# Moving the clipped decay difference of a Mamba-2 scan from ScalarE to VectorE

## The chip, the cores and the metric

The kernel runs on one core of a Trainium2 chip, as one launch. The metric is the device time in microseconds (us). A core has five engines that run side by side and wait for each other through counters (semaphores): PE (TensorE, matrix products), DVE (VectorE), ACT (ScalarE), POOL (GpSimd) and SP (SyncE, which here only starts transfers). SBUF is the working memory with 128 partitions; PSUM holds the results of PE in eight banks, which DVE and ACT can read.

## The reference

One inference step of a two-layer decoder for 256 prompt tokens and 8 decode tokens: an attention layer with a dense SwiGLU, then a Mamba-2 layer with a mixture of 8 experts. The change touches only the chunked scan of the Mamba-2 layer, for the prompt: two chunks of 128 tokens, 32 heads in 4 groups of 8.

```python
cum = jnp.cumsum(jnp.moveaxis(dtf * a_neg.reshape(g, hg), 2, -1), axis=-1)
causal = jnp.tril(jnp.ones((cl, cl), dtype=bool))
seg = jnp.exp(jnp.where(causal, cum[..., :, None] - cum[..., None, :], -jnp.inf))
xdt = xf * dtf[..., None]
cb = jnp.einsum('bclgn,bcsgn->bcgls', cf, bf)
y_diag = jnp.einsum('bcghls,bcsghp->bclghp', cb[:, :, :, None] * seg, xdt)
...
y_off = jnp.einsum('bclgn,bcghpn,bcghl->bclghp', cf, h_in, jnp.exp(cum))
```

`seg` is a 128 x 128 matrix for each head and chunk: e to the power of cum(l) - cum(s) where l is not before s, and 0 elsewhere. As the sums fall with time, the difference is never positive where it counts. So the kernel clips it at 0, takes the exponential, and leaves the masking to the product with `cb`, which is masked already.

## The kernel before, in words

All data are 32-bit floats. The Mamba-2 scan is the function `group(g_)` on DVE (line 1983), a loop over `g_` on ACT (line 1581) and one on PE (line 1108), each run four times, once for a group of 8 heads. The order on each engine is written out by hand, and each engine works strictly in that order. The loop index `n` counts 16 blocks, four in each group; a block is one chunk of one half group, so four heads, and its matrices are 128 x 512.

For a block, PE spreads the running sums of four heads over all partitions into bank 6 or bank 2 (line 1134; it counts `cum_spread`). ACT then computes max(cum(s) - cum(l), 0) with four Relu instructions of 128 x 128, one for each head, since each has its own column of `wtok` as the bias (line 1589; `seg_min`). It then takes Exp with scale -1 over the whole block (line 1594; `seg_exp`). For each odd block it also takes Exp of bank 2 (line 1598; `ecum_exp`), which PE needs before that bank can be filled again. DVE multiplies the block by the masked `cb` into `gseg` (line 2003, in `weigh(n)`), and after each odd block also forms `coff` (line 2006).

In each group DVE first scales the tokens into `xdt` (line 1992, five of them) and copies two results of PE out of bank 7 (lines 1996 and 1997). Then come the four `weigh(n)`. Between and behind them stand calls of `state_output(n)`: each is two products (line 1964) and two reductions (line 1965), of 128 x 512, for the decode tokens. There are 4, 6, 6 and 0 of these calls in groups 0 to 3. The group ends with four instructions on line 2041 and one on line 2049, which wait for the two `y_done` of PE. The first `state_output` also waits for the transfers of the rows `srow` and `feat` (`rows_spread`).

PE, in each group, turns tokens (line 1114, which waits for `y_ready` of the group before, that is for line 2041 on DVE), computes `cb` (lines 1117 and 1119), spreads the sums of two blocks (line 1134), computes one output chunk of z (line 1066, 16 products), spreads the sums of the other two blocks, forms the states (lines 1141 to 1148), computes the next z chunk, then y in two halves (lines 1161 to 1163; each half waits for its `seg_ready` and `coff_ready` from DVE, the first also for `hin` from ACT), and computes a last z chunk. ACT takes the SiLU of each z chunk (line 1559, in `z_act`). After group 3 come the output projection (line 991), the norm, the router and the experts (lines 1320 to 1374), whose weights SP brings into a ring of tiles; SP waits for PE to free a tile (line 518).

In ACT's rows a table load stands wherever the function changes between Silu and Exp. The profile names `dseg`, `eseg` and `gseg` as `segs`, `coff` and `ecum` as `convbuf`, and `hin` as `dtbuf`, as these are views of those tiles.

Of the kernel before, what the change touches and what calls it, by code (L numbers as in the profile page):

```python
# [15 lines left out]
ALU = mybir.AluOpType  # L16
ACT = mybir.ActivationFunctionType
# [3 lines left out]
P = 128  # L21
# [18 lines left out]
HG = SH // SG  # L40
# [129 lines left out]
def build(nc, a, o):  # L170
# [116 lines left out]
    wtok = sb("wtok", [P, 9, SH], c=c3)  # L287
# [1127 lines left out]
    def _(act):  # L1415
        f = act.activation
# [160 lines left out]
        f(decay, decay, ACT.Exp).then_inc(s["us_silu"], 1)  # L1577
        act.wait_ge(s["xs_turned"], 1)
        f(xtok, bank[2][:, 0:P], ACT.Copy).then_inc(s["xs_copied"], 1)
        act.wait_ge(s["out_done"], 112)  # L1580
        for g_ in range(SG):
            for n in range(4 * g_, 4 * g_ + 4):
                half, t = (n % 4) // 2, n % 2
                act.wait_ge(s["cum_spread"], n + 1)
                if n >= 2:
                    act.wait_ge(s["seg_exp"], n - 1)
                for q in range(4):
                    hh = HG * g_ + 4 * half + q
                    ins = f(dseg[:, n % 2, q, :], bank[(6, 2)[t]][:, q * P:(q + 1) * P], ACT.Relu, bias=wtok[:, 5 + t, hh:hh + 1], scale=-1.0)
                ins.then_inc(s["seg_min"], 1)  # L1590
                if n >= 2:
                    act.wait_ge(s["seg_ready"], n - 1)
                act.wait_ge(s["seg_min"], n + 1)
                f(eseg[:, n % 2], dseg[:, n % 2], ACT.Exp, scale=-1.0).then_inc(s["seg_exp"], 1)
                if n % 2:
                    if n > 1:
                        act.wait_ge(s["coff_ready"], n // 2)
                    f(ecum, bank[2][:].rearrange("p (q t) -> p q t", q=4), ACT.Exp).then_inc(s["ecum_exp"], 1)
                if n % 4 == 1:
                    z_act(*Z_AMID[g_][0])  # L1600
            act.wait_ge(s["carry_done"], 2 * g_ + 1)
            f(hin, bank[7][:], ACT.Copy).then_inc(s["hin_copied"], 1)
            act.wait_ge(s["carry_done"], 2 * g_ + 2)
            if g_:
                act.wait_ge(s["hlast_out"], 16 * g_)
            f(hout, bank[3][:].rearrange("p (q n) -> p q n", q=4), ACT.Copy).then_inc(s["hlast_copied"], 1)
            act.wait_ge(s["hlast_copied"], g_ + 1)
            act.dma_start(o[6][0, 0, HG * g_:HG * (g_ + 1)].rearrange("(q j) p n -> (j p) q n", j=2), hout).then_inc(s["hlast_out"], 16)
            z_act(*Z_AMID[g_][1])
            z_act(*Z_AMID[g_][2])  # L1610
            act.wait_ge(s["zy_ready"], g_ + 1)
            for c in range(4 * g_, 4 * g_ + 4):
                ins = f(sz[:, c, 0:TP], xcT[:, c, 0:TP], ACT.Copy, scale=vec[:, V_SNG + c:V_SNG + c + 1])
            ins.then_inc(s["gained"], 1)
# [69 lines left out]
    def _(v):  # L1684
# [298 lines left out]
        def group(g_):  # L1983
# [13 lines left out]
            v.tensor_tensor(cbT, bank[7][:, 2 * P:4 * P].rearrange("p (t n) -> p t n", t=2), mid(cst[:, C_U:C_U + P], 2), ALU.mult).then_inc(s["cb_ready"], 1)  # L1997
            v.wait_ge(s["cb_ready"], g_ + 1)

            def weigh(n):  # L2000
                half, t = (n % 4) // 2, n % 2
                v.wait_ge(s["seg_exp"], n + 1)
# [3 lines left out]
                    v.tensor_tensor(coff[:, half], ecum, mid(bcT[:, SG + g_, P:TP], 4), ALU.mult).then_inc(s["coff_ready"], 1)  # L2006

            n0 = 4 * g_
            if g_ == 0:
                weigh(n0)  # L2010
                weigh(n0 + 1)
                for n in range(3):
                    state_output(n)
                weigh(n0 + 2)
# [2 lines left out]
            elif g_ < 3:  # L2017
                state_output(6 * g_ - 2)
                weigh(n0)
                state_output(6 * g_ - 1)  # L2020
                weigh(n0 + 1)
                state_output(6 * g_)
                weigh(n0 + 2)
                weigh(n0 + 3)
# [6 lines left out]
                    v.tensor_tensor(ysp[:], ysp[:], bc(decay, [P, NB, IC]), ALU.mult).then_inc(s["ys_ready"], 1)  # L2031
            else:
                weigh(n0)
                weigh(n0 + 1)
                weigh(n0 + 2)
                weigh(n0 + 3)
            for half in range(2):
# [276 lines left out]
```

## Time and profile before

| what | value |
|---|---|
| median of 3 runs | 1746.16 us (1738.31 to 1746.92) |
| profiled execution, its own time | 1746.16 us |
| span of the profiled execution | 1744.6 us |
| PE busy | 1638.3 us (94%) |
| DVE busy | 420.6 us (24%) |
| ACT busy | 277.4 us (16%) |
| share of the last chain of work | PE 85%, DVE 7%, DMA 3%, ACT 2% |

The span is what the trace covers; 1.6 us of the execution lie around it. "Busy" is the time in which an engine worked on an instruction. The granted clock is the part of full speed that PE was given: 1.00 is 2.4 GHz and 0.50 is 1.2 GHz. The four groups of the scan lie between about 749 and 861 us of the span.

### The profile page before, as it was taken

The page shows a single profiled execution, that of the slowest core. Times are in us where ns is not written, and L with a number is a line of the kernel's source. Part 1 is how long each engine was busy: PE and PEld are TensorE (multiplying, and loading weights), DVE is VectorE, ACT ScalarE, POOL GpSimd, SP SyncE. Part 2 cuts the span into 40 slices and gives each one's busy share as a digit, 9 for nine tenths or more (in the row PEclk, how much of TensorE's full clock was granted, in tenths as well). Part 3 has the DMA queues.
Part 4 walks back from the last instruction along what each step waited for, and adds up shares of the span by engine and source line. Part 5 has one row for each costly group of instructions (what it writes and reads, how often), then busy time and mean ns, then how long its engine had stood idle before and what let it go on. Part 6 is the DMA issues. An engine that isn't in the chain of part 4 may idle for free.

```text
span 1744.6 us, 20839 instructions
## 1 busy us (share of the span) xinstructions
PE 1638.3 (94%) x8060; PEld 1042.4 (60%) x8060; DVE 420.6 (24%) x984; ACT 277.4 (16%) x615; POOL 112.8 (6%) x190
## 2 busy tenths in 40 slices
PE   7999897799999999998898999999999999999993
PEld 4555563478888878787786544554445454544452
DVE  2233432220000035679556100010001000010002
ACT  2212322210000022345413000000000000100001
POOL 0001404100000010020011000000000000010001
PEclk9999998899999999989899799999999999999996
DMA  9655974154433564545269699999999999999996
GB/s 357 259 185 195 317 246 114 34 177 144 145 115 118 173 210 124 154 126 181 77 223 361 223 335 387 386 383 388 381 393 387 379 379 394 384 380 389 392 387 232
DMA packets 255210, 462.88 MB, mean 265 GB/s; under 512 B 13423, under 2 KB 112780, under 8 KB 252005
## 3 DMA queue, kind: packets, MB, share of 16 engines
q1 hardware_dynamic: 240848, 415.02, 66.7%
q0 software_dynamic: 11760, 45.38, 8.2%
q8 instruction: 64, 1.05, 0.2%
q10 hardware_dynamic: 2512, 1.23, 0.2%
q14 instruction: 26, 0.21, 0.0%
HBM read 445.15 MB, written 16.63 MB: 265 GB/s over the span
## 4 chain that ended last, share of the span: by engine, by line
PE 85%; DVE 7%; DMA 3%; issue 2%; ACT 2%; SPq 1%; POOLq 0%; POOL 0%; DVEq 0%; ACTq 0%
PE bank L1320 18%; PE bank L991 10%; PE bank L1362 9%; PE bank L1018 9%; PE bank L1335 9%; PE bank L1374 5%; PE bank L1032 5%; PE bank L731 2%; PE bank L821 1%; PE bank L768 1%; PE bank L739 1%; DVE ysp L1965 1%; DVE prod L1964 1%; PE bank L1066 1%; PE bank L826 1%
## 5 line engine op out<-in xcount | busy, mean ns | idle before, releaser
L1320 PE MATMUL bank<-ring,hg 128*128 128x512 f32 (+1 forms) x624 | 254.7, 566 | 0.7 <-ACT hg L1645 0.7
L1320 PEld LDWEIGHTS bank<-ring,hg 128*128 128x128 f32 x624 | 119.1, 192 | 132.0 <-issue 129.6
L1018 PE MATMUL bank<-hT,ring 128*128 128x264 f32 x704 | 156.9, 386 | 1.3 <-ACT hT L1431 1.3
L1018 PEld LDWEIGHTS bank<-hT,ring 128*128 128x128 f32 x704 | 133.7, 190 | 24.9 <-issue 2.1
L2228 DVE TENSOR_TENSOR actH<-sgH,bank 128x512 f32<-128x512 f32 (+1 forms) x24 | 15.4, 643 | 465.7 <-PE bank L1320 465.7
L1362 PE MATMUL bank<-ring,turnH 128*128 128x512 f32 x256 | 115.8, 605 | 3.3 <-ACT turnH L1670 3.3
L991 PE MATMUL bank<-hT,ring 128*128 128x264 f32 x512 | 117.4, 390 | 1.6 <-ACT hT L1431 1.3
L991 PEld LDWEIGHTS bank<-hT,ring 128*128 128x128 f32 x512 | 98.2, 192 | 19.6 <-issue 2.1
L1335 PE MATMUL bank<-ringx,hg 128*64 128x256 f32 x832 | 93.0, 381 | 0.0
L1362 PEld LDWEIGHTS bank<-ring,turnH 128*128 128x128 f32 x256 | 47.9, 192 | 68.7 <-issue 67.8
L1032 PE MATMUL bank<-actT,ring 128*128 128x264 f32 x352 | 79.1, 386 | 0.6 <-DVE actT L1868 0.6
L1335 PEld LDWEIGHTS bank<-ringx,hg 128*64 128x64 f32 x832 | 58.5, 137 | 32.2 <-issue 4.1
L1032 PEld LDWEIGHTS bank<-actT,ring 128*128 128x128 f32 x352 | 66.8, 190 | 12.4 <-DVE actT L1868 1.0
L1658 ACT ACTIVATE sgH<-bank 128x512 f32<-128x512 f32 (+1 forms) x24 | 13.5, 562 | 374.9 <-PE bank L1320 374.9
L1374 PE MATMUL bank<-ring,turnL 128*64 128x512 f32 x288 | 67.7, 612 | 0.8 <-DVE turnL L2244 0.8
L1335 PE MATMUL bank<-ring,hg 128*64 128x256 f32 (+1 forms) x704 | 65.0, 342 | 0.0
L1066 PE MATMUL bank<-hT,ring 128*128 128x264 f32 x256 | 64.9, 412 | 0.0
L991 PE MATMUL bank<-sz,ring 128*128 128x264 f32 x256 | 60.0, 394 | 3.6 <-DVE sz L2060 3.6
L1066 PEld LDWEIGHTS bank<-hT,ring 128*128 128x128 f32 x256 | 51.1, 204 | 10.6 <-issue 1.4
L991 PEld LDWEIGHTS bank<-sz,ring 128*128 128x128 f32 x256 | 49.7, 194 | 12.8 <-DVE sz L2060 4.0
L1320 PE MATMUL bank<-ringx,hg 128*128 128x512 f32 (+1 forms) x144 | 56.4, 545 | 0.0
L1665 ACT ACTIVATE sgL<-bank 128x256 f32<-128x256 f32 (+1 forms) x24 | 8.8, 366 | 298.1 <-PE bank L1335 298.1
(509 smaller groups left out, 1846.5 us busy)
## 6 DMA issues: line engine op xcount, KB each, us to landing
ring<-in_moe_w_down SPq DMA_DIRECT2D x70, 1024.0 KB, 12.7
ring<-in_moe_w_up SPq DMA_DIRECT2D x59, 1024.0 KB, 11.4
ring<-in_moe_w_gate SPq DMA_DIRECT2D x55, 1024.0 KB, 11.5
ring<-in_w_ada SPq DMA_DIRECT2D x48, 1024.0 KB, 8.9
ringx<-in_moe_w_gate SPq DMA_DIRECT2D x37, 1024.0 KB, 11.0
ringx<-in_moe_w_up SPq DMA_DIRECT2D x33, 1024.0 KB, 12.0
ring<-in_ssm_w_in SPq DMA_DIRECT2D x20, 1024.0 KB, 5.3
ringx<-in_moe_w_down SPq DMA_DIRECT2D x20, 1024.0 KB, 12.3
```

What stands on the lines that cost most here:

```text
L731: m = mm(b_[rows, :], scT[:, 4 * u + k, :], slot4(n + u)[:, k, :], start=u == 0, stop=u == 1, skip_group_check=True)
L739: m = mm(out[q], adaS[:, u, q * P:(q + 1) * P], cst[:, C_SEL:C_SEL + 9], start=True, stop=True)
L768: m = mm(out, slot8(n)[:, k, (m_ % 2) * P:(m_ % 2) * P + width], hT[:, k, :], start=k == 0, stop=k == DC - 1)
L821: m = mm(bank[h % 2][0:QK, 0:T], wqb[:, k, h * QK:(h + 1) * QK], projT[:, k, :], start=k == 0, stop=k == QC - 1)
L991: m = mm(bank[n % 4][:, 0:T], w[:, k, (n % per_tile) * P:(n % per_tile + 1) * P], rhs[:, k, :], start=k == 0, stop=k == kc - 1)
L1018: m = mm(bank[2 * w + q][:, 0:T], slot8(tl)[:, k, q * P:(q + 1) * P], hT[:, k, :], start=k == 0, stop=k == DC - 1)
L1032: m = mm(bank[2 * (j % 2) + q][:, 0:T], slot8(tl)[:, kk, q * P:(q + 1) * P], actT[:, k0 + kk, :], start=k == 0 and kk == 0, stop=k == 3 an ...
L1066: m = mm(bank[n % 2][:, 0:T], slot8(tl)[:, k, (n % 2) * P:(n % 2 + 1) * P], hT[:, k, :], start=k == 0, stop=k == DC - 1)
L1320: m = mm(bank[b_][:, 0:width], hg[:, k, 0:CAPH], w[:, kk, :], start=k == 0, stop=k == DC - 1)
L1335: m = mm(bank[2][64 * v_:64 * v_ + 64, 256 * b_:256 * b_ + width // 2], hg[:, k, CAPH:CAPS], w[:, kk, v_], start=k == 0, stop=k == DC - 1, ...
L1362: m = mm(bank[4 + half][:, :], turnH[:, 2 * i + q, :], w[:, q, 512 * half:512 * (half + 1)], start=g == 0 and i == 0 and q == 0, stop=g == ...
L1374: m = mm(bank[6][64 * v_:64 * v_ + 64, :], turnL[:, i, 64 * q:64 * q + 64], w[:, q, 512 * v_:512 * (v_ + 1)], start=g == 0 and i == 0 and ...
```

## The change

The clipped difference goes from ACT to DVE. ACT loses its 64 Relu instructions and waits for `seg_min` from DVE; its Exp no longer has the scale -1, as DVE writes min(cum(l) - cum(s), 0). ACT's one wait for `out_done` goes too; DVE has the same wait ahead of its first group. DVE gains a function `seg(n)` with four TENSOR_SCALAR instructions of 128 x 128 from PSUM (subtract a column of `wtok`, then min with 0), and each group calls it four times: for the first two blocks behind line 1997, for the third behind the first `weigh`, for the fourth behind the second `weigh`. The waits on `cum_spread` and on `seg_exp` (of two blocks before) go with it to DVE.

```diff
@@ ACT
-        act.wait_ge(s["out_done"], 112)
         for g_ in range(SG):
             for n in range(4 * g_, 4 * g_ + 4):
-                half, t = (n % 4) // 2, n % 2
-                act.wait_ge(s["cum_spread"], n + 1)
-                if n >= 2:
-                    act.wait_ge(s["seg_exp"], n - 1)
-                for q in range(4):
-                    hh = HG * g_ + 4 * half + q
-                    ins = f(dseg[:, n % 2, q, :], bank[(6, 2)[t]][:, q * P:(q + 1) * P], ACT.Relu, bias=wtok[:, 5 + t, hh:hh + 1], scale=-1.0)
-                ins.then_inc(s["seg_min"], 1)
+                act.wait_ge(s["seg_min"], n + 1)
                 if n >= 2:
                     act.wait_ge(s["seg_ready"], n - 1)
-                act.wait_ge(s["seg_min"], n + 1)
-                f(eseg[:, n % 2], dseg[:, n % 2], ACT.Exp, scale=-1.0).then_inc(s["seg_exp"], 1)
+                f(eseg[:, n % 2], dseg[:, n % 2], ACT.Exp).then_inc(s["seg_exp"], 1)
@@ DVE
+            def seg(n):
+                half, t = (n % 4) // 2, n % 2
+                v.wait_ge(s["cum_spread"], n + 1)
+                if n >= 2:
+                    v.wait_ge(s["seg_exp"], n - 1)
+                for q in range(4):
+                    hh = HG * g_ + 4 * half + q
+                    ins = v.tensor_scalar(dseg[:, n % 2, q, :], bank[(6, 2)[t]][:, q * P:(q + 1) * P], wtok[:, 5 + t, hh:hh + 1], 0.0,
+                                          ALU.subtract, ALU.min)
+                ins.then_inc(s["seg_min"], 1)
...
             n0 = 4 * g_
+            seg(n0)
+            seg(n0 + 1)
             if g_ == 0:
                 weigh(n0)
+                seg(n0 + 2)
                 weigh(n0 + 1)
+                seg(n0 + 3)
                 for n in range(3):
                     state_output(n)
                 weigh(n0 + 2)
...
             elif g_ < 3:
                 state_output(6 * g_ - 2)
                 weigh(n0)
+                seg(n0 + 2)
                 state_output(6 * g_ - 1)
                 weigh(n0 + 1)
+                seg(n0 + 3)
                 state_output(6 * g_)
...
             else:
                 weigh(n0)
+                seg(n0 + 2)
                 weigh(n0 + 1)
+                seg(n0 + 3)
                 weigh(n0 + 2)
                 weigh(n0 + 3)
```

PE's order is the same in both. On DVE in group 0, from the last copy out of bank 7 to the first `state_output` (lines 1964 and 1965), stands before:

```order
L1997 TENSOR_TENSOR usbuf<-bank,cst 128x256
L2003 TENSOR_TENSOR segs<-segs,usbuf 128x512 [waits seg_exp,cb_ready]
L2003 TENSOR_TENSOR segs<-segs,usbuf 128x512 [waits seg_exp]
L2006 TENSOR_TENSOR convbuf<-convbuf,bcT 128x512 [waits ecum_exp]
L1964 TENSOR_TENSOR prod<-st,srow 128x512 [waits st_loaded0,rows_spread]
L1965 TENSOR_REDUCE ysp<-prod 128x4 [waits dve_step]
```

In the changed kernel (where line 1998 is `seg`, 2005 and 2008 are `weigh`, 1955 and 1956 are `state_output`) the same place reads:

```order
L1988 TENSOR_TENSOR usbuf<-bank,cst 128x256
L1998 TENSOR_SCALAR segs<-bank,wtok 128x128 [waits cum_spread,cb_ready]
L1998 TENSOR_SCALAR segs<-bank,wtok 128x128 x3
L1998 TENSOR_SCALAR segs<-bank,wtok 128x128 [waits cum_spread]
L1998 TENSOR_SCALAR segs<-bank,wtok 128x128 x3
L2005 TENSOR_TENSOR segs<-segs,usbuf 128x512 [waits seg_exp]
L1998 TENSOR_SCALAR segs<-bank,wtok 128x128 [waits seg_exp,cum_spread]
L1998 TENSOR_SCALAR segs<-bank,wtok 128x128 x3
L2005 TENSOR_TENSOR segs<-segs,usbuf 128x512 [waits seg_exp]
L2008 TENSOR_TENSOR convbuf<-convbuf,bcT 128x512 [waits ecum_exp]
L1998 TENSOR_SCALAR segs<-bank,wtok 128x128 [waits seg_exp,cum_spread]
L1998 TENSOR_SCALAR segs<-bank,wtok 128x128 x3
```

All four `seg` now stand ahead of the first `state_output`, and the last two wait for the third and fourth `cum_spread` of PE.

On ACT in group 0, from the SiLU of a z chunk on, stands before:

```order
L1559 ACT_TABLE_LOAD
L1559 ACTIVATE sz<-bank 128x264 [waits units]
L1589 ACTIVATE segs<-bank,wtok 128x128 [waits seg_exp,cum_spread]
L1589 ACTIVATE segs<-bank,wtok 128x128 x3
L1594 ACT_TABLE_LOAD [waits seg_min]
L1594 ACTIVATE segs<-segs 128x512 [waits seg_ready]
L1589 ACTIVATE segs<-bank,wtok 128x128 [waits seg_exp,cum_spread]
L1589 ACTIVATE segs<-bank,wtok 128x128 x3
L1594 ACTIVATE segs<-segs 128x512 [waits seg_min,seg_ready]
```

and in the changed kernel (line 1585 is the Exp):

```order
L1559 ACT_TABLE_LOAD
L1559 ACTIVATE sz<-bank 128x264 [waits units]
L1585 ACT_TABLE_LOAD [waits seg_ready]
L1585 ACTIVATE segs<-segs 128x512 [waits seg_min]
L1585 ACTIVATE segs<-segs 128x512 [waits seg_ready,seg_min]
```

The number of table loads is the same; the load for Exp no longer waits for `seg_min`.

## Rows read from the trace of the kernel before

**Rows 1.** Stretches of the four groups: busy time (instructions) by engine, PE clock, DMA

```profile
749.00:777.00 28.00, 27.57 (x161) 23.33 (x160) 21.44 (x34) 13.70 (x30) 6.57 (x11) 0.82 0.55 143
777.00:805.00 28.00, 23.50 (x164) 20.02 (x162) 26.84 (x43) 16.77 (x37) 1.59 (x3) 0.97 0.60 190
805.00:833.00 28.00, 24.10 (x162) 20.52 (x161) 26.96 (x43) 16.63 (x35) 1.44 (x2) 0.93 0.36 117
833.00:861.00 28.00, 27.54 (x157) 23.00 (x155) 9.47 (x18) 16.81 (x35) 0.55 (x1) 0.80 0.18 50
```

**Rows 2.** Timeline of DVE, group 2: start, us, operation, [idle before]

```profile
811.59 0.69 DVE L2003 TENSOR_TENSOR segs<-segs,usbuf 128x512 f32<-128x512 f32 x1
812.20 0.68 DVE L1964 TENSOR_TENSOR prod<-st,srow 128x512 f32<-128x512 f32 x1
```

**Rows 3.** Waits from 745 to 875 us: what for, us in total, times, longest

```profile
DVE segs L2003 <- ACT segs L1594: 15.1, 6, 6.3
```

**Rows 4.** Timeline of DVE, groups 0 and 3

```profile
757.25 0.68 DVE L2006 TENSOR_TENSOR convbuf<-convbuf,bcT 128x512 f32<-128x512 f32 x1
760.44 0.69 DVE L1964 TENSOR_TENSOR prod<-st,srow 128x512 f32<-128x512 f32 x1 [2.51 <-DMA feat<-xsd]
...
777.24 3.08 DVE L1992 TENSOR_TENSOR xdt<-bank,wtok 128x512 f32<-128x512 f32 x5 [0.50 <-PE bank L1114]
...
851.95 0.68 DVE L2006 TENSOR_TENSOR convbuf<-convbuf,bcT 128x512 f32<-128x512 f32 x1
```

**Rows 5.** Timeline of PE, groups 0 to 3

```profile
760.55 2.05 PE L1134 MATMUL bank<-feat,cst 32*128 32x128 f32 x16
...
770.35 0.38 PE L1163 MATMUL bank<-convbuf,dtbuf 128*64 128x128 f32 x2
771.16 0.40 PE L1161 MATMUL bank<-segs,xdt 128*64 128x128 f32 x2 [0.43 <-DVE convbuf L2006]
...
772.87 3.83 PE L1066 MATMUL bank<-hT,ring 128*128 128x264 f32 x16
...
803.69 1.97 PE L1114 MATMUL bank<-cst,xcT 128*128 128x128 f32 x8 [4.50 <-DVE xcT L2041]
...
831.81 1.97 PE L1114 MATMUL bank<-cst,xcT 128*128 128x128 f32 x8 [3.90 <-DVE xcT L2041]
...
838.69 6.61 PE L1066 MATMUL bank<-hT,ring 128*128 128x264 f32 x16
845.23 2.04 PE L1134 MATMUL bank<-feat,cst 32*128 32x128 f32 x16
849.95 3.73 PE L1066 MATMUL bank<-hT,ring 128*128 128x264 f32 x16
```

**Rows 6.** Timeline of ACT, groups 0 and 2

```profile
761.74 1.14 ACT L1589 ACTIVATE segs<-bank,wtok 128x128 f32<-128x128 f32 x4 [0.69 <-PE bank L1134]
...
816.25 1.28 ACT L1594 ACT_TABLE_LOAD   x1
```

**Rows 7.** Groups of DVE instructions by shape: busy us, mean ns, idle before

```profile
L1896 DVE TENSOR_SCALAR dtbuf<-bank,hp_ 32x264 f32<-32x264 f32 x1 | 0.5, 480 | 1.1 <-PE bank L1051 1.1
```

**Rows 8.** Timeline of DVE: rows that give a step from start to start

```profile
830.10 1.65 DVE L2041 SCALAR_TENSOR_TENSOR xcT<-xcT,expd,bank 128x256 f32<-128x256 f32 x4
...
991.38 0.28 DVE L2159 TENSOR_SCALAR pick<-cst,slots 128x128 f32<-128x128 f32 x1
991.58 0.28 DVE L2160 TENSOR_SCALAR pick<-twice,slots 128x128 f32<-128x128 f32 x1
```

**Rows 9.** PE in three stretches: length, busy (instructions), granted clock, DMA

```profile
800.00:812.00 12.00, 8.31 (x44) 0.86 0.62 203
828.00:848.00 20.00, 16.19 (x64) 0.66 0.11 26
862.00:872.00 10.00, 7.87 (x28) 0.83 0.56 176
```

**Rows 10.** Waits of SP's queue from 700 us: us in total, times, longest

```profile
SPq L518 <- PE bank L1320: 248.3, 86, 15.6
```

## The prediction

> **What bounds the kernel now.** I first read the busy times by stretch. The page of the profile calls PE 94% busy and DVE 24%, but that is a mean over stages. In the stretches of groups 1 and 2 of the scan, DVE works 26.84 and 26.96 of 28 us while PE works 23.50 and 24.10, and ACT 16.77 and 16.63 [rows 1]. So there DVE sets the pace. In group 3, where no decode work stands on DVE, it is PE: 27.54 of 28 us, with DVE at 9.47.
>
> Next I read DVE's timeline, to see whether "busy" hides waits. In group 2 the first weigh starts at 811.59 and the next instruction at 812.20, 0.61 us on and with no idle time before it [rows 2]. The waits confirm it: over all four groups DVE stood before line 2003 only six times, 15.1 us in all [rows 3]. On the timeline two of them lie in group 0 and four in group 3, none in groups 1 and 2. Group 0 is different: DVE finishes its first coff at 757.93, then waits 2.51 us for a transfer, and starts the first state_output at 760.44 [rows 4].
>
> Then PE's timeline. In group 0 it waits for DVE's second coff and starts the second half of y at 771.16. In groups 2 and 3 it opens only after 4.50 and 3.90 us of waiting for DVE's line 2041 [rows 5]. Behind the scan, SP waits for PE to free ring tiles, 86 times for line 1320 alone, 248.3 us in total [rows 10]. The experts are thus not fed too slowly: they start late if PE comes late, and nothing behind makes it up. A delay of the scan should reach the end one for one.
>
> **The change, part by part.** ACT loses 64 Relu of 128 x 128; four of them take 1.14 us [rows 6], so about 18 us of busy time. I count that as no gain: ACT has 11 us of slack in each group [rows 1], and neither PE nor DVE waits for it in groups 1 and 2. ACT's dropped wait for the output transfers costs or gains nothing, since its first Relu waited for PE beyond it and DVE holds the same wait already. The table loads stay in number; they now precede the wait for DVE and so lie beside its work.
>
> DVE gains 64 TENSOR_SCALAR of 128 x 128 from PSUM with a scalar column. The trace has no such shape; I need the step from one start to the next. Above: 256 columns from PSUM with a scalar column take 1.65 us for four, 0.41 a step [rows 8]. The column price is (690 - 280)/384 = 1.07 ns, from 512 columns at 0.69 us [rows 2] and 128 at 0.28 us [rows 8]. So 128 columns fewer make 0.41 - 0.137 = 0.27. Second way: the same operation from PSUM, 264 columns, lasts 480 ns [rows 7]; less 136 columns that is 0.335. The 128-column row shows steps of 0.20 at a duration of 0.28 [rows 8], so a step is 0.08 below the duration: 0.255. Below lies the SBUF step itself, 0.20. I take 0.26, from the same operation, so 1.04 us for one seg (0.80 to 1.34 with the full duration as the step).
>
> On that last bound the Trainium skill bears ("VectorE: DVE Perf Modes", section "The DRAIN you can't avoid"): the next operation does not start until the pipe is empty. By that a seg would cost four durations, 1.34 us. The trace of before speaks against it for unchained operations, with 0.20 from start to start at a duration of 0.28 [rows 8].
>
> Group 0. seg of blocks 0 and 1 fits into DVE's old wait for ACT. The third seg needs PE's third spread: ACT's Relu on it started at 761.74, having waited for PE [rows 6], and PE's sixteen products there run from 760.55 to 762.60 [rows 5]. PE gets there no sooner. On DVE's queue this wait now holds up the weigh and coff of block 1, the fourth seg, and all state_outputs. So: seg at 761.74, to 762.78; weigh and coff at 0.61 each, to 764.00; fourth seg to 765.04. The first state_output starts there and not at 760.44: +4.60 us. The transfer it waited for [rows 4] has landed by then. Everything DVE does in the group follows, then PE's second half of y, then PE's transposes. DVE waited 0.50 us for these before 777.24 [rows 4], so PE is last there and the delay passes on whole.
>
> Groups 1 and 2. Each has four seg on a DVE without idle time: 4 x 1.04 = 4.16 us each, +8.32. No wait comes with them: PE is ahead of DVE there, as its 4 us of slack show [rows 1], and ACT finishes each Exp behind a 2.9 us state_output.
>
> Group 3. Four more seg, 4.16 us, but hidden. PE ends its middle z chunk at 849.95 + 3.73 = 853.68 [rows 5], DVE its last coff before at 852.63 [rows 4]. With the change: third spread done at about 846.25 [rows 5], seg 847.3, weigh and coff 848.5, fourth seg 849.6, Exp 850.3, then weigh and coff to 851.6. That is 2 us before PE needs it; if the cover went it would cost up to 4.2.
>
> PE's clock. PE's wait before the second half of y in group 0 grows from 0.43 us to 775.76 - 770.73 = 5.0 us [rows 5]. Around the waits of 4.50 and 3.90 us, and one after 860 us, the mean granted clock was 0.86 over 12 us, 0.66 over 20 and 0.83 over 10 [rows 9]. As only 0.50 and 1.00 occur, that is 3.4, 13.6 and 3.4 us at 1.2 GHz. So I expect a slow stretch behind the new wait. A short one takes at most 3.4/2 = 1.7 us from the work that follows, part of it falling into the wait; I take 1.1, and it is exposed, since PE is last there. Group 3 I leave as it was.
>
> This is also what the Trainium skill says ("TensorE: Matmul & The Clock Gate", "Part 1: The HAM clock gate"): throttled is the default, and activity releases it. The trace agrees in all three places above.
>
> Sum: 4.60 + 8.32 + 1.1 = 14.0 us. The profiled execution took 1746.16 us, 1.6 over its span of 1744.6, and is the median of the three runs itself. So 1760 us, +0.8%. The third run, at 1738.31, shows that one execution can come out 8 us shorter.
>
> **The rivals.**
> A, a long slow clock behind the new wait: 13.6 us as in group 3 instead of 3.4. PE's work from 771.16 to 776.7 (half of y, a z chunk) then takes twice as long, +5.4 in place of 1.1, giving 12.9 + 5.4 = 18.3 us, 1764 us. For it: 16 products of line 1066 took 6.61 us in group 3 and 3.73 at full clock [rows 5]. Against: two of three stretches were short.
>
> B, the clock goes the other way: group 3 opens with a short slow stretch where before it had the long one. PE sets the pace there, so (13.6 - 3.4)/2 = 5.1 us come back; with seg at 0.80 the DVE terms are 4.12 + 6.40. Then 10.5 + 1.1 - 5.1 = 6.5 us, 1753 us. For it: when the clock falls and returns differs from gap to gap. Against: it takes both.
>
> C, the delay is taken up later: prefetch stands full anyway, or a later wait for a transfer shrinks by as much. That would be 1747 to 1750 us. Against: SP's waits for PE [rows 10].
>
> D, ACT paces the groups and DVE's state_outputs only fill: then each of groups 0 to 2 loses two Relu blocks (2 x 1.14 us) and one exposed table load (1.28) [rows 6], 3.56 us each, 10.7 together: 1735.5 us, faster. It decides if DVE waits for Exp inside groups 1 and 2. Against: all its waits there are in groups 0 and 3 [rows 3], and the starts stand back to back [rows 2].
>
> E, the pipe empties between the seg instructions: 1.34 us a seg. Group 0 costs 2.52 + 2.68 = 5.2, groups 1 and 2 10.7, with the clock 17.0 us, 1763 us. The skill's page on draining would have it so.
>
> **How the numbers follow.** Forecast 0.55 (its own range 1756 to 1763), A 0.13, B 0.12, C 0.07, D 0.05, E 0.08. Half a per cent is 8.7 us, about what a measurement of this kernel can tell from no change; so slower means above 1754.9. Slower: 0.55 + 0.13 + 0.08 and a third of B, 0.80. Same: the rest of B and C, 0.15. Faster: D, 0.05. The range, 1751 to 1767 us, runs from just below B to above A and E, and leaves out C and D, and the case that A and E come together with more waits.
>
> **What would show it.** DVE's line 1998: 64 instructions, 0.33 to 0.35 us each, four in about 1.1. The first state_output near 765.0. PE's second half of y in group 0 near 775.8, with about 5 us of idle time before it. Groups 1 and 2 together longer by 8.3 us, and DVE without idle time in both. Group 3 no longer than before but for its clock. The forecast is wrong if DVE shows idle time inside groups 1 and 2, if a step is under 0.20, if PE arrives in group 0 earlier than at 760.55, or if the experts begin less late than the scan ends late.

## The result, and the profile after

The changed kernel took 1754.56 us in the median of its 17 runs (1748.22 to 1759.22), against 1745.25 us for 17 runs of the kernel before on the same chip, one of which came out at 1963.56 us and is left out of the comparison. The ratio is 1.0059, with a 95% interval of [1.0045, 1.0075]: the change makes the kernel slower, by 0.59% or 10.3 us (0.0059 x 1745; the medians as they stand are 9.3 apart). In a later series the same pair gave 1756.94 us (4 runs) and 1743.94 us (23 runs), a ratio of 1.0081 [1.005, 1.0112]. The prediction was 1760 us, in a range from 1751 to 1767.

The profiled execution has a span of 1755.5 us, against 1744.6 before. Its busy times and its instructions, from the page:

```profile
PE 1636.9 (93%) x8060; PEld 1042.4 (59%) x8060; DVE 437.4 (25%) x1048; ACT 260.7 (15%) x551; POOL 112.9 (6%) x190
```

DVE gained 64 instructions and 16.8 us, ACT lost 64 and 16.7 us. That says nothing of the path. The next view is the busy times of the four groups, each from DVE's first `xdt` to that of the next group (columns: stretch, length, then PE, PEld, DVE, ACT, POOL with their instructions, granted clock, DMA share, GB/s):

```profile
748.40:782.80 34.40, 29.40 (x163) 24.88 (x162) 25.56 (x50) 9.58 (x15) 6.59 (x11) 0.80 0.46 134
782.80:814.60 31.80, 23.65 (x162) 19.88 (x161) 30.87 (x58) 12.28 (x19) 1.59 (x3) 0.98 0.49 147
814.60:846.70 32.10, 24.70 (x162) 20.86 (x161) 31.11 (x60) 12.47 (x19) 1.44 (x2) 0.93 0.34 103
846.70:874.50 27.80, 27.23 (x157) 22.76 (x155) 13.63 (x34) 12.48 (x19) 0.55 (x1) 0.81 0.18 50
```

In groups 1 and 2, DVE is busy for 30.87 of 31.80 and 31.11 of 32.10 us, so it still sets the pace and every added us lengthens them. In group 3, PE is busy for 27.23 of 27.80, as before [rows 1]. Group by group, between the same landmarks on DVE's timeline (from the first `xdt` to that of the next group; group 3 ends where DVE's last product over 1024 columns of `xcT` and `sz` starts, at 861.07 us before and 874.46 after):

| us | group 0 | group 1 | group 2 | group 3 | sum |
|---|---|---|---|---|---|
| before | 28.21 | 27.68 | 28.11 | 28.04 | 112.04 |
| after | 34.40 | 31.81 | 32.06 | 27.76 | 126.03 |
| difference | +6.19 | +4.13 | +3.95 | -0.28 | +13.99 |

DVE's timeline, groups 0 and 1 (start, us, operation, idle time before it in brackets), shows how these come about:

```profile
761.14 1.13 DVE L1998 TENSOR_SCALAR segs<-bank,wtok 128x128 f32<-128x128 f32 x4 [5.30 <-PE bank L1134]
762.18 0.68 DVE L2005 TENSOR_TENSOR segs<-segs,usbuf 128x512 f32<-128x512 f32 x1
762.78 0.69 DVE L2008 TENSOR_TENSOR convbuf<-convbuf,bcT 128x512 f32<-128x512 f32 x1
763.38 1.12 DVE L1998 TENSOR_SCALAR segs<-bank,wtok 128x128 f32<-128x128 f32 x4
764.42 0.68 DVE L1955 TENSOR_TENSOR prod<-st,srow 128x512 f32<-128x512 f32 x1
...
782.83 3.08 DVE L1983 TENSOR_TENSOR xdt<-bank,wtok 128x512 f32<-128x512 f32 x5 [2.13 <-PE bank L1114]
...
786.60 2.16 DVE L1998 TENSOR_SCALAR segs<-bank,wtok 128x128 f32<-128x128 f32 x8
788.68 0.68 DVE L1955 TENSOR_TENSOR prod<-st,srow 128x512 f32<-128x512 f32 x1
```

The first `state_output` starts at 764.42, where before it stood at 760.44 [rows 4]. PE's third spread came 0.60 us sooner in this execution (759.95 against 760.55 [rows 5]), so against PE the delay is 3.98 + 0.60 = 4.6 us. Eight clip instructions in a row take 788.68 - 786.60 = 2.08 us from start to start, which is 0.26 us each, or 1.04 a `seg`. At the end of group 0, DVE waits 2.13 us for PE's transposes where it had waited 0.50 [rows 4]. PE's timeline of that place says why:

```profile
759.95 2.04 PE L1134 MATMUL bank<-feat,cst 32*128 32x128 f32 x16
...
775.13 0.40 PE L1161 MATMUL bank<-segs,xdt 128*64 128x128 f32 x2 [5.00 <-DVE convbuf L2008]
...
778.01 4.27 PE L1066 MATMUL bank<-hT,ring 128*128 128x264 f32 x16
782.12 1.04 PE L1114 MATMUL bank<-cst,xcT 128*128 128x128 f32 x8
```

PE waited 5.00 us instead of 0.43 and then worked at a lower clock for a while: the z chunk behind it took 4.27 us and not 3.83 [rows 5], and the half of y before it from 775.13 to 778.01, 2.88 us, against 772.87 - 771.16 = 1.71 before. The granted clock of two stretches there, and of one in group 3:

```profile
772.00:776.00 4.00, 0.87 (x10) 0.90 (x12) 3.90 (x7) 0.00 (x0) 0.00 (x0) 0.94 1.04 362
776.00:780.00 4.00, 4.00 (x25) 3.38 (x22) 3.86 (x8) 0.00 (x0) 0.55 (x1) 0.63 0.21 33
848.00:852.00 4.00, 4.00 (x19) 3.78 (x19) 3.57 (x9) 1.72 (x4) 0.55 (x1) 0.50 0.05 16
```

With 0.50 and 1.00 as the only levels, the first two hold (0.06 + 0.37) x 8 = 3.4 us at 1.2 GHz. That stretch costs 1.6 us (2.13 - 0.50, and 1.17 + 0.44 on PE). It began only when PE was at work again: from 775.0 to 775.5 us the granted clock was still 1.00, from 775.6 to 778.9 it was 0.50. The waits from 745 to 875 us (us in total, times, longest) have the new ones:

```profile
ACT segs L1585 <- DVE segs L1998: 27.5, 14, 5.6
...
DVE segs L1998 <- PE bank L1134: 12.3, 5, 5.6
...
PE bank L1161 <- DVE convbuf L2008: 7.7, 3, 5.0
...
PE bank L1161 <- ACT dtbuf L1593: 3.3, 2, 2.2
```

The last two rows also hold waits of PE inside groups 1 and 2 which the kernel before did not have: 2.17 and 1.16 us for ACT's `hin`, and 1.35 us in each for DVE's `coff`. They cost nothing, since DVE is last in these groups.

In group 3 the clip waits for PE's third spread too, as ACT's did before, but nothing is late behind it. DVE and then PE at that place:

```profile
859.81 1.13 DVE L1998 TENSOR_SCALAR segs<-bank,wtok 128x128 f32<-128x128 f32 x4 [5.61 <-PE bank L1134]
...
864.48 0.68 DVE L2008 TENSOR_TENSOR convbuf<-convbuf,bcT 128x512 f32<-128x512 f32 x1
```

```profile
845.48 1.97 PE L1114 MATMUL bank<-cst,xcT 128*128 128x128 f32 x8 [4.88 <-DVE xcT L2051]
...
863.34 3.73 PE L1066 MATMUL bank<-hT,ring 128*128 128x264 f32 x16
```

DVE ends its last `coff` at 865.16, PE its middle z chunk at 867.07: 1.9 us of slack. The kernel before had 1.05 there (852.63 against 853.68): with the clip on DVE, the last `coff` is done 18.5 us after the group's start and not 19.6.

Behind the scan the two executions differ once more. The span grew by 10.9 us and not by 14. The scan started 0.6 us sooner, and what lies behind it took 2.5 us less. The kernel before had two stretches of 3.4 us at 1.2 GHz in its experts and the changed one had none; at half their length they make up 3.4 us, so 0.9 us went the other way and were not traced. The 16 products of line 1362 hold the first of these stretches; PE in the kernel before, and after:

```profile
991.46 8.63 PE L1362 MATMUL bank<-ring,turnH 128*128 128x512 f32 x16 [0.88 <-ACT turnH L1670]
```

```profile
1004.83 7.11 PE L1362 MATMUL bank<-ring,turnH 128*128 128x512 f32 x16 [0.88 <-ACT turnH L1661]
```

These products start 1004.83 - 991.46 = 13.37 us later, and the scan ended 874.46 - 861.07 = 13.39 us later: up to there nothing made the delay up.

### The profile page after: what moved, and what is told of

It reads as the page before. It is cut to its first block, busy times and chain, and to the rows that moved or that the text cites. A ratio compares the mean times of both kernels' runs of the same rounds, so it can differ in the third digit from the quotient of the medians.

```text
span 1755.5 us, 20835 instructions
## 1 busy us (share of the span) xinstructions
PE 1636.9 (93%) x8060; PEld 1042.4 (59%) x8060; DVE 437.4 (25%) x1048; ACT 260.7 (15%) x551; POOL 112.9 (6%) x190
## 3 DMA queue, kind: packets, MB, share of 16 engines
q8 instruction: 64, 1.05, 0.3%
## 4 chain that ended last, share of the span: by engine, by line
PE 86%; DVE 8%; DMA 2%; issue 2%; ACT 1%; SPq 1%; POOLq 0%; POOL 0%; DVEq 0%; ACTq 0%
PE bank L1320 17%; PE bank L991 10%; PE bank L1018 9%; PE bank L1362 9%; PE bank L1335 9%; PE bank L1374 5%; PE bank L1032 4%; PE bank L731 2%; PE bank L821 1%; PE bank L768 1%; PE bank L1066 1%; DVE ysp L1956 1%; DVE prod L1955 1%; PE bank L739 1%; PE bank L826 1%
## 5 line engine op out<-in xcount | busy, mean ns | idle before, releaser
L2238 DVE TENSOR_TENSOR actH<-sgH,bank 128x512 f32<-128x512 f32 (+1 forms) x24 | 15.4, 644 | 463.7 <-PE bank L1320 463.7
L991 PEld LDWEIGHTS bank<-hT,ring 128*128 128x128 f32 x512 | 98.2, 192 | 19.6 <-issue 2.1
L1335 PEld LDWEIGHTS bank<-ring,hg 128*64 128x64 f32 x704 | 45.5, 137 | 17.6 <-issue 2.3
## 6 DMA issues: line engine op xcount, KB each, us to landing
ringx<-in_moe_w_up SPq DMA_DIRECT2D x33, 1024.0 KB, 13.6
ringx<-in_moe_w_down SPq DMA_DIRECT2D x20, 1024.0 KB, 13.7
```

What stands on the lines that cost most here:

```text
L991: m = mm(bank[n % 4][:, 0:T], w[:, k, (n % per_tile) * P:(n % per_tile + 1) * P], rhs[:, k, :], start=k == 0, stop=k == kc - 1)
L1335: m = mm(bank[2][64 * v_:64 * v_ + 64, 256 * b_:256 * b_ + width // 2], hg[:, k, CAPH:CAPS], w[:, kk, v_], start=k == 0, stop=k == DC - 1, ...
```

## The experiments

The kernels marked with "before" start from the kernel before, the others from the changed one. Ratios are taken against the kernel before in the same batch, on the same chip (1744.82 us for x1, x2, x3 and y1, 1743.19 for x6, b2, x9 and y4, 1743.94 for w1 and y5), so kernels of different batches are better compared by their ratios. The lengths of the groups, from the profile of each, in the same way as above:

| kernel | group 0 | group 1 | group 2 | group 3 | sum | median us | ratio |
|---|---|---|---|---|---|---|---|
| x1_order | 30.20 | 31.73 | 32.06 | 28.08 | 122.07 | 1751.5 | 1.0041 [1.0024, 1.0057] |
| x2_act12 | 34.38 | 27.59 | 28.09 | 23.48 | 113.54 | 1742.54 | 0.9987 [0.9962, 1.0012] |
| x3_keep | 33.55 | 31.71 | 31.96 | 22.14 | 119.36 | 1749.53 | 1.0027 [1.0013, 1.0041] |
| y1_shift (before) | 29.69 | 24.70 | 24.69 | 22.66 | 101.74 | 1729.45 | 0.9911 [0.9882, 0.9939] |
| x6_g3 | 29.67 | 27.62 | 28.07 | 23.39 | 108.75 | 1743.1 | 1.0003 [0.9981, 1.0025] |
| b2_keep (before) | 28.39 | 27.60 | 27.85 | 22.20 | 106.04 | 1733.38 | 0.9935 [0.9912, 0.9958] |
| x9_double | 34.30 | 35.96 | 38.15 | 27.69 | 136.10 | 1765.01 | 1.0124 [1.009, 1.0158] |
| y4_keep (before) | 31.37 | 24.70 | 24.69 | 22.51 | 103.27 | 1729.89 | 0.9919 [0.9892, 0.9947] |
| w1_both | 31.36 | 28.81 | 28.80 | 28.18 | 117.15 | 1742.56 | 0.9992 [0.997, 1.0014] |
| y5_out (before) | 29.82 | 24.68 | 24.68 | 22.54 | 101.72 | 1732.76 | 0.9925 [0.9899, 0.995] |

### Group 0: the wait alone (x1_order)

The same work, with the third and fourth `seg` later on DVE's queue:

```diff
                 weigh(n0)
-                seg(n0 + 2)
                 weigh(n0 + 1)
+                state_output(0)
+                seg(n0 + 2)
+                state_output(1)
                 seg(n0 + 3)
-                for n in range(3):
-                    state_output(n)
+                state_output(2)
```

> Changed kernel with another order on DVE in group 0 alone: both weigh first, then state_output(0), the third seg, state_output(1), the fourth seg, state_output(2). If the 4.6 us of group 0 are a wait for PE's third spread (2.5 us) plus two seg (2.08 us), only the two seg remain: the first state_output starts when its transfer has landed, 4.0 us earlier than in the changed kernel, DVE has no 5.3 us of idle time before a seg there, group 1 starts 2.5 us earlier, and the time is about 1752 us. If group 0 costs by DVE's load alone, the order changes nothing and the time stays at 1754.5.

Group 0 fell from 34.40 to 30.20 us, by 4.2. DVE and PE at the same places:

```profile
757.05 0.69 DVE L1955 TENSOR_TENSOR prod<-st,srow 128x512 f32<-128x512 f32 x1 [2.49 <-DMA feat<-xsd]
...
759.95 1.13 DVE L1998 TENSOR_SCALAR segs<-bank,wtok 128x128 f32<-128x128 f32 x4
...
775.91 3.08 DVE L1983 TENSOR_TENSOR xdt<-bank,wtok 128x512 f32<-128x512 f32 x5 [0.50 <-PE bank L1114]
```

```profile
769.84 0.40 PE L1161 MATMUL bank<-segs,xdt 128*64 128x128 f32 x2 [1.36 <-DVE convbuf L2008]
...
771.54 3.83 PE L1066 MATMUL bank<-hT,ring 128*128 128x264 f32 x16
```

`seg` no longer waits, DVE is back at the old 2.49 us of waiting for the transfer, PE waits 1.36 us in place of 5.00, and its z chunk takes 3.83 us. So 2.5 us of group 0's 6.2 were the wait, 1.6 the clock behind PE's wait, and the 2.0 that stay (30.20 - 28.21) are the two `seg` that no cover hides.

### Groups 1 and 2: the work alone (x2_act12, x9_double)

x2_act12 gives the clip of groups 1 and 2 back to ACT, with the wait on `cum_spread` and the four Relu as they were before:

```diff
             for n in range(4 * g_, 4 * g_ + 4):
+                on_act = g_ in (1, 2)
+                if on_act:
...
             def seg(n):
+                if g_ in (1, 2):
+                    return
```

> Changed kernel with the clip of groups 1 and 2 back on ACT as Relu; groups 0 and 3 stay on DVE. If the 32 seg instructions of groups 1 and 2 lie on the path at 0.26 us each, 8.3 us go: about 1746 us, and each of the two groups takes 4.16 us less. If DVE's load there is hidden and the loss comes from group 0 or from PE's clock, the time stays at 1751 us or above.

Both groups returned to their old lengths, by 4.22 and 3.97 us. The row of group 1 is that of before again, with DVE at 26.68 of 27.60 us and ACT at 16.48:

```profile
782.90:810.50 27.60, 23.04 (x163) 19.56 (x161) 26.68 (x42) 16.48 (x35) 1.59 (x3) 0.99 0.55 169
...
838.60:862.10 23.50, 22.95 (x157) 19.41 (x155) 13.51 (x34) 12.47 (x19) 0.55 (x1) 0.96 0.20 59
```

Group 3 was 4.3 us shorter than after, with a granted clock of 0.96 in place of 0.81: the slow stretch at its opening was a short one here. That is rival B's event, and it was not asked for. The median fell by 12 us where 8.3 were expected, and the profile shows where the rest can come from: 4.3 us in group 3, and 4.4 us behind the scan, where a slow stretch of 17.1 us at the router, which both kernels of the pair had, was missing. So the lengths of groups 1 and 2 are the evidence here, and not the median.

x9_double has DVE do each clip of groups 1 and 2 a second time, into `gseg`, which is overwritten later:

```diff
                                           ALU.subtract, ALU.min)
+                if g_ in (1, 2):
+                    for q in range(4):
+                        hh = HG * g_ + 4 * half + q
+                        ins = v.tensor_scalar(gseg[:, half, t, q, :], bank[(6, 2)[t]][:, q * P:(q + 1) * P], wtok[:, 5 + t, hh:hh + 1], 0.0,
+                                              ALU.subtract, ALU.min)
```

> Changed kernel with each clip instruction of groups 1 and 2 issued twice on DVE, the second time into a buffer that is written again before it is read. If these instructions lie on the path at 0.26 us each, both groups get another 4.16 us longer: 1754.5 + 8.3 = 1763 us. If the loss came from waits and order and not from load, the time stays near 1755.

Group 1 grew by 4.15 us, as much as the first clip had cost. Group 2 grew by 6.09. The windows of its opening and rest:

```profile
812.00:828.00 16.00, 13.19 (x46) 11.27 (x46) 15.24 (x35) 6.01 (x9) 0.53 (x1) 0.57 0.41 133
828.00:854.00 26.00, 17.00 (x121) 14.10 (x120) 23.84 (x47) 6.46 (x10) 1.44 (x2) 0.95 0.31 92
```

A slow stretch of 13.7 us now stood at the opening of group 2 as well, where the changed kernel had one of 3.4; group 3 kept its own (27.69 us, granted clock 0.81). PE had four us of slack in group 2 and used them up; DVE then waited 1.50 us for PE's spread, which with the 4.16 of work makes 5.66 of the 6.09 us:

```profile
829.37 1.13 DVE L1998 TENSOR_SCALAR segs<-bank,wtok 128x128 f32<-128x128 f32 x4 [1.50 <-PE bank L1134]
```

### Group 3 and the clock (x6_g3, x3_keep, b2_keep, y4_keep)

x6_g3 has the clip on DVE in group 3 alone, and on ACT in groups 0 to 2 (and keeps ACT's wait for `out_done`).

```diff
+                on_act = g_ < 3
+                if on_act:
...
+            def seg(n):
+                if g_ < 3:
+                    return
```

> Kernel before with the clip on DVE in group 3 alone (16 of the 64 instructions), groups 0 to 2 as before. If group 3 hides them behind PE, groups 0 to 2 last as before, group 3 lasts 28.0 us at the long slow clock or some 23 us at a short one, and the time is that of the kernel before, about 1745 us. If they lie on the path, group 3 gets up to 4.2 us longer: 1749 us.

The median did not change (1.0003). Group 3 took 23.39 us, again with a short slow stretch, so its length can't be set beside 28.04. The next two can: in both, PE does unused products of 128 x 512 (line 705) while it would wait. x3_keep, on the changed kernel:

```diff
                 if t == 0 and g_ > 0:
+                    pe.wait_ge(s["seg_min"], 4 * g_)
+                    keep_clock(bank[6], 5)
                     pe.wait_ge(s["y_ready"], 2 * g_)
...
             for half in range(2):
+                if g_ == 0 and half:
+                    pe.wait_ge(s["seg_min"], 4)
+                    keep_clock(bank[6], 5)
                 pe.wait_ge(s["seg_ready"], 4 * g_ + 2 * half + 2)
```

> Changed kernel in which PE runs five unused 128 x 512 products (about 4.6 us) before it waits for DVE: in group 0 ahead of the second half of y, and at the start of groups 1 to 3. They write a free bank and are read by nobody. If the clock terms are as worked out, the granted clock stays at 1.00 through the scan, the first xdt scaling of group 1 comes 1.6 us earlier, and group 3, which PE paces, gets 5 to 6 us shorter: about 1747 us in all. If the clock costs nothing there, since DVE is last anyway, the time stays at 1754.5; if the extra products come in the way of the real ones, it rises by 1 to 3 us.

b2_keep, on the kernel before, has four of them at the opening of groups 2 and 3 only:

```diff
+                if t == 0 and g_ > 1:
+                    pe.wait_ge(s["seg_min"], 4 * g_)
+                    keep_clock(bank[6], 4)
                 if t == 0 and g_ > 0:
```

> Kernel before in which PE runs four unused 128 x 512 products (about 3.6 us) before it waits for DVE at the start of groups 2 and 3, into a free bank. If the slow clock at the start of group 3 costs 5 us of a stretch that PE paces, group 3 gets 5 us shorter and the time is about 1740 us; groups 0 to 2 stay as they are, since DVE paces them. If the clock is not on the path, the time stays at 1745 us.

Group 3, first in x3_keep, then in b2_keep:

```profile
840.50:862.60 22.10, 21.62 (x153) 18.13 (x151) 13.49 (x34) 12.47 (x19) 0.55 (x1) 1.00 0.23 64
```

```profile
827.90:850.10 22.20, 21.66 (x153) 18.18 (x151) 9.46 (x19) 16.65 (x35) 0.55 (x1) 1.00 0.24 64
```

At full clock throughout, group 3 lasts 22.14 us with the clip on DVE and 22.20 with it on ACT. So the clip of group 3 costs nothing, which is shown here with PE at its fastest. The slow stretch of group 3 cost 28.04 - 22.20 = 5.8 us in the kernel before and 27.76 - 22.14 = 5.6 in the changed one, nearly as much as the change cost in group 0.

In group 0, x3_keep gained only 0.85 us, where its expectation had more. The products at the opening of group 1 stood in the way:

```profile
771.84 4.45 PE L705 MATMUL bank<-cst 128*128 128x512 f32 x10
776.13 1.04 PE L1116 MATMUL bank<-cst,xcT 128*128 128x128 f32 x8
```

There PE is last, and the transposes (line 1116 here) started 4.3 us later than they could. Two gains stand against this loss. The clock behind the second half of y gave its 1.6 us. And PE's third spread started 8.00 us after the first `xdt` and not 11.52, because in this execution the slow stretch at the start of the scan, which the edit doesn't touch, was 3.4 us long and not 10.2; that took 3.5 us off. The edit was misplaced by me; it tells nothing against the clock. y4_keep repeats the error in small. It adds to y1_shift (below) four unused products before the second half of y in group 0 and three before the output projection:

```diff
+                if g_ == 0 and half:
+                    pe.wait_ge(s["seg_min"], 4)
+                    keep_clock(bank[6], 4)
...
+        keep_clock(bank[6], 3)
         pe.wait_ge(s["gated_vector"], 1)
```

> The kernel with 4, 5, 5 and 2 calls of state_output, and unused products on PE where it still waits: four ahead of the second half of y in group 0, three ahead of the output projection. In the run without them one slow stretch of 3.4 us stood behind each of these two waits. If both cost half their length, 3.4 us go: about 1726 us. If one of them was hidden, half of that; if neither costs, 1729.5.

It stayed level with y1_shift (1729.89 and 1729.45 us). PE's products ran from 770.76 to 774.46, while DVE's `coff` was ready at 771.14 already:

```profile
770.76 3.70 PE L705 MATMUL bank<-cst 128*128 128x512 f32 x8
774.39 0.43 PE L1164 MATMUL bank<-segs,xdt 128*64 128x128 f32 x2
```

```profile
770.45 0.69 DVE L2010 TENSOR_TENSOR convbuf<-convbuf,bcT 128x512 f32<-128x512 f32 x1
```

Group 0 took 31.37 us, against 29.69 in y1_shift. But y4_keep had the 10.2 us stretch at the start of the scan and y1_shift one of 3.4; with the long one, group 0 took 28.1 to 28.4 us in the kernels before without the insertion (profiles of before, r_before and b2_keep), so the insertion cost about 3. The equal medians hide more than this: behind the scan the profiled execution of y4_keep was 7.5 us shorter (its slow stretch at the router was 3.4 us long and not 17.1), and 4.2 us of its time lay outside the span, where y1_shift had 1.6. So this run says nothing of the second insertion. y5_out drops the first of the two insertions and keeps `keep_clock(bank[6], 3)` before the projection.

> The kernel with 4, 5, 5 and 2 calls of state_output and three unused products on PE ahead of its wait before the output projection, where nothing real is held up. The first two columns of the projection took 9.06 us behind a slow clock and 7.1 at full clock: about 2 us less than without them, 1727.5 us, if the clock stays up; 1729.5 if not. Groups 0 to 3 as in the kernel without them, 101.7 us.

The products fit into PE's wait, and the projection's first 32 products took 7.38 us, against 9.07 in y1_shift. PE in y5_out, then in y1_shift:

```profile
850.40 2.74 PE L705 MATMUL bank<-cst 128*128 128x512 f32 x6
854.16 7.38 PE L991 MATMUL bank<-sz,ring 128*128 128x264 f32 x32 [1.02 <-DVE sz L2062]
```

```profile
848.87 9.07 PE L991 MATMUL bank<-sz,ring 128*128 128x264 f32 x32 [3.59 <-DVE sz L2061]
```

No gain is left in the time: 1732.76 us where 1727.5 were expected, with a ratio whose interval overlaps that of y1_shift. In this profile the slow stretch at the router was 20.5 us long instead of 17.1, which by half of 3.4 would take the 1.7 us back; whether the one brought the other wasn't tried.

### The better versions (y1_shift, w1_both)

If DVE paces groups 1 and 2 and PE group 3, decode work should move from the former to the latter. y1_shift is the kernel before with 4, 5, 5 and 2 `state_output` in the groups, in place of 4, 6, 6 and 0; the scaling of `ysp` goes from the end of group 2 to behind the last of them:

```diff
             elif g_ < 3:
-                state_output(6 * g_ - 2)
+                first = 5 * g_ - 1
+                state_output(first)
...
-                state_output(6 * g_ + 3)
             else:
+                state_output(14)
                 weigh(n0)
                 weigh(n0 + 1)
+                state_output(15)
+                v.wait_ge(s["ys_ready"], NB)
...
```

> Kernel before with 4, 5, 5 and 2 calls of state_output in groups 0 to 3 in place of 4, 6, 6 and 0. If DVE's load sets the length of groups 1 and 2, each gets 2.9 us shorter and the two calls in group 3 are hidden beside PE: 5.8 us less, about 1739.5 us, and up to 5 more where PE's wait gets too short to drop the clock for group 3. If ACT or PE paces the groups, the time stays at 1745.

Groups 1 and 2 fell by 2.98 and 3.42 us, one `state_output` each (2.9 us; group 2 also lost the scaling of `ysp`), and group 3 by 5.4: PE's waits before groups 2 and 3 shrank to 1.61 and 1.74 us, and no slow stretch followed them.

```profile
797.34 1.09 PE L1114 MATMUL bank<-cst,xcT 128*128 128x128 f32 x8 [1.61 <-DVE xcT L2042]
...
822.03 1.09 PE L1114 MATMUL bank<-cst,xcT 128*128 128x128 f32 x8 [1.74 <-DVE xcT L2042]
```

This is the fastest kernel of the study, 0.9911 [0.9882, 0.9939] of the kernel before. w1_both puts the clip on DVE in it, with group 0 in the order of x1_order.

> The kernel with 4, 5, 5 and 2 calls of state_output and with the clip on DVE (in group 0 in the better order). If the clip costs wherever DVE paces, groups 1 and 2 last 24.7 + 4.2 = 28.9 us each and group 0 gains 2.1; in group 3, where DVE now has two state_outputs as well, up to 4 us are no longer hidden: 10 to 14 us over the 1729.5 of the kernel without the clip on DVE, so 1740 to 1744 us. If relief of ACT is worth something once DVE has less to do, it stays under 1737.

Its median is 13 us above that of y1_shift (14 by the ratios), and its scan is 15.4 us longer: 1.7, 4.1, 4.1 and 5.5 in the four groups. Group 3 is no longer free, because the clip now delays the last decode results on DVE, and PE waits for their transfer, 2.52 us where y1_shift waits 0.4, with a slow stretch behind it (5.42 us for 16 products, 3.73 in y1_shift):

```profile
854.78 0.33 PE L1167 MATMUL bank<-cst,usbuf 128*128 128x128 f32 x1 [2.52 <-DMA usbuf<-ysd]
854.95 5.42 PE L1066 MATMUL bank<-hT,ring 128*128 128x264 f32 x16
```

### The pair once more (r_after, r_before)

Both kernels unchanged, in a series of their own.

> The changed kernel once more, for a second profile. Its four groups lasted 126.0 us in the first, 14.0 more than before, but the time rose by only 10.3. If the scan differs from execution to execution by the length of PE's slow stretches, the sum of groups 0 to 2 stays within 2 us of 98.3, as DVE paces them, and group 3 is either near 28 or near 23 us. If the 14 us were a chance of one profile, the groups 1 and 2 move too.

> The kernel before once more, for a second profile. Groups 1 and 2 stay at 27.7 and 28.1 us, group 0 at 28 to 30, group 3 near 28 or near 23 us by the length of the slow stretch at its start.

The scan took 125.89 and 112.05 us, a difference of 13.84 (6.19, 4.12, 3.92 and -0.39 by group). In this pair neither execution had a slow stretch in the experts, and nothing was given back there: the spans, 1750.5 and 1744.6, differ by 5.9 us, and this is 13.84 less the 7.9 us by which the scan began earlier in r_after (743.65 against 751.59). The medians, 1756.94 and 1743.94, are 13.0 apart. The kernel before under its own label, r_before, gave 1744.57 us in 10 runs, a ratio of 0.9998 [0.9978, 1.0018] to itself.

## Why the prediction was right

**The bound.** DVE paces groups 1 and 2, PE group 3, and nothing behind the scan makes a delay up. The first two held. x2_act12 takes the work of groups 1 and 2 away and gets 4.22 and 3.97 us for 4.16; x9_double doubles it and gets 4.15 in group 1, and 6.09 in group 2, where a long slow stretch of PE joined in. The third held in the two profiled pairs: the experts began 13.37 us later where the scan ended 13.39 later, and in the second pair what lies behind the scan took the same time in both. Over all runs it isn't shown, as the time below says.

**Group 0, 4.60 us.** Measured 4.6, counted from PE's third spread, and x1_order splits it: moving `seg` behind work that needs nothing of PE takes the 2.5 us of waiting away and leaves 2.0, two `seg` on the path.

**Groups 1 and 2, 8.32 us.** Measured 4.13 + 3.95 = 8.08. The step is 0.26 us, while one instruction lasts 342 ns (mean of the 64). The low bound, 0.20, and rival E, a whole duration for each, are both refuted. (The section of the Trainium skill that the prediction cites beside E goes on to say that an instruction which is not held starts earlier; the steps here agree with that part of it.) The prediction expected no new wait in these groups; there were some on PE, up to 2.17 us, and DVE being last hid them.

**Group 3, nothing.** Measured -0.28, with 1.9 us of slack where the working had 2. At full clock, 22.14 against 22.20.

**The clock, 1.1 us.** The stretch came where it was forecast and with the length of 3.4 us, behind a wait of 5.00 us. It cost 1.6: the working let part of it fall into the wait, but it began 0.4 us behind the wait and lay wholly on work. This is the one term of the sum that was mis-sized by more than its rounding, by 0.5 us, and the short 8.08 and the -0.28 of group 3 balanced it. That the sum came out to the tenth is partly luck.

**The time.** So the scan grew by 13.99 us where the sum had 14.0. The time grew by less: by 10.3 us in the first series, with an interval of 7.9 to 13.1 that leaves 14.0 out, and by 13.0 in the second (8.7 to 19.5). The forecast of 1760 is 5.4 us above the first median of 1754.56. What took the 3.7 us of the first series back is open. A part can be estimated from the mean granted clock that is recorded for every run: it makes 130.6 us at 1.2 GHz in the mean of 22 runs of the changed kernel, and 131.1 in 76 of the kernel before (standard errors 1.5 and 0.8). So over many runs the changed kernel had no clear surplus of slow time, though both its profiles have 3.4 us more in group 0; it seems to have less of it elsewhere, which at half of 3.4 would be 1.7 us. The 2.5 us that the first profiled pair gave back behind the scan look like rival C, but its mechanism was not seen: the experts began as late as the scan ended, two slow stretches of PE were missing in one execution, and in the second pair they were missing from both. As such stretches and the start of the scan (743.3 to 751.6 us over the profiles, with kernels that are equal up to there) vary from one execution to the next, one pair of profiles can't give the difference of the medians to better than some us: what lies behind the scan took 876.3 us in the profile of x6_g3 and 883.5 in that of the kernel before, with the same work in it. Rival A, a slow stretch of 13.6 us behind PE's wait in group 0, didn't occur in any profile; the longest there was 6.8, in w1_both. Rival B's short stretch did, in x2_act12 and x6_g3. Rival D fell with x2_act12: ACT with the clip does the groups in their old time and no faster.

On the clock the Trainium skill ("TensorE: Matmul & The Clock Gate", section "Part 1: The HAM clock gate") has activity release the throttle. x3_keep and b2_keep agree: with unused products in the waits, the stretches from group 1 to group 3 were all at 1.00.

What stays open: y1_shift and b2_keep gained 15 and 10 us in the median of 6 and 10 runs, against 10.3 and 6.0 in the scan of their profiles. Their profiles lack the two stretches of 3.4 us in the experts too, but so does that of r_before, and whether these kernels avoid them was not settled. For the runs of b2_keep, 1.6 to 3.3 us of the time lie outside the span, where the kernel before has 1.6 in each; why was not looked into. Nor is it known what decides between a slow stretch of 3.4 and one of 13.7 us at the opening of group 3: the waits before it were 3.90 us in the kernel before and 3.72 in x2_act12.

## What to carry to other kernels

Ask of each stage which engine is last in it, and price moved work there: the same 4.2 us of clips cost 4.2 where DVE was last, nothing where PE was, and 6.2 where they also brought a wait to the head of a queue. Then turn the finding round: work that may be done in any stage belongs to the stage in which its engine isn't last, which here was worth 15 us in the median (10.3 in the scan of the profile, and 5.4 of those by the clock of group 3), more than the change cost. In front of an engine whose clock falls, a wait costs more than its length, and filling it with unused work pays only if that work ends before the wait would have.

## What the runs showed of the hardware

A slow stretch of PE's clock doesn't end when work resumes. Behind the 4.88 us wait at group 3 of the changed kernel, PE was busy for 11.90 of 11.90 us (845.5 to 857.4) and still had a granted clock of 0.50; the stretch lasted 13.7 us and cost 5.6. Its neighbours behind waits of 5.00 and 4.63 us, in groups 0 and 2, lasted 3.4 us. Nor does it always begin in the wait: in y1_shift PE resumed at 766.05 us, the granted clock was 1.00 up to 767 us and 0.50 from 767.3 to 770.5.

A faster PE can lose time by it. In x6_g3 and y1_shift the slow stretch that begins shortly ahead of the scan was 6.8 and 3.4 us long, against 10.2 in the kernel before; PE reached the second half of y sooner, waited there 4.3 and 3.8 us instead of 0.43, fell to 1.2 GHz again behind the wait, and group 0 was 1.5 us longer than before. The profile of y5_out repeats it (3.4 us, a wait of 3.90, 29.82 us), and the profiles of r_before and b2_keep, with 10.2 us at the start, took 28.13 and 28.39.
